# Thirty-two batches of unread one-pass products behind the first 32 rows of a modulation matrix

## The reference

```python
c_act = jax.nn.silu(c)
mod = c_act @ ada_w[l] + ada_b[l]
sh1, sc1, g1, sh2, sc2, g2 = jnp.split(mod, N_MOD, axis=-1)
h = rms_norm(x, mix_pre_g[l]) * (1.0 + sc1[:, None, :]) + sh1[:, None, :]
y = hybrid_mixer(h, w_in[l], conv_w[l], ...)
x = x + g1[:, None, :] * rms_norm(y, mix_post_g[l])
h = rms_norm(x, ffn_pre_g[l]) * (1.0 + sc2[:, None, :]) + sh2[:, None, :]
y = swiglu_ffn(h, w_gate[l], w_up[l], w_down[l])
x = x + g2[:, None, :] * rms_norm(y, ffn_post_g[l])
```

## Time and profile before

| | |
|---|---|
| median of 2 runs | 2617.11 us (2616.35 to 2617.87) |
| span of the profiled execution | 2614.0 us |
| TensorE matmul busy | 2567.3 us, 98% |
| VectorE, ScalarE, GpSimd busy | 1691.6, 1222.0, 49.9 us |
| read from HBM | 541.78 MB, mean 208 GB/s |

### The profile page before, as it was taken

One profiled execution on the slowest core, in us unless ns is written; L12 is line 12 of the kernel. 1 busy time (PEld: TensorE's weight loads), 2 busy tenths in 40 slices (PEclk: granted clock), 3 DMA queues, 4 the chain that ended last, 5 costly groups with the idle time before them and its releaser, 6 DMA issues.

```text
span 2614.0 us, 54085 instructions
## 1 busy us (share of the span) xinstructions
PE 2567.3 (98%) x21414; PEld 2438.5 (93%) x21414; DVE 1691.6 (65%) x2347; ACT 1222.0 (47%) x1667; POOL 49.9 (2%) x98
## 2 busy tenths in 40 slices
PE   5999999999999999999999999999999999999999
PEld 1488889999999999999999999999999999999999
DVE  1388867686666666557655655554766776666667
ACT  1343455554444444446545444444544444444445
POOL 0000000000000000000000000000000000000000
PEclk9899999999999999999999999999999999999999
DMA  9988868466666666554544455555455555555554
GB/s 390 383 322 306 289 210 311 168 204 226 224 226 225 226 224 209 183 192 161 170 145 139 151 176 179 188 178 187 151 187 186 188 187 185 187 186 188 186 186 138
DMA packets 136065, 545.53 MB, mean 209 GB/s; under 512 B 15121, under 2 KB 15377, under 8 KB 123537
## 3 DMA queue, kind: packets, MB, share of 16 engines
q1 hardware_dynamic: 126288, 474.08, 54.1%
q0 software_dynamic: 9216, 67.11, 7.2%
q10 hardware_dynamic: 448, 2.75, 0.3%
HBM read 541.78 MB, written 2.10 MB: 208 GB/s over the span
## 4 chain that ended last, share of the span: by engine, by line
PE 94%; DMA 2%; DVE 2%; ACT 1%; issue 0%; ACTq 0%; DVEq 0%; SPq 0%
PE bank L1797 20%; PE bank L1799 20%; PE bank L1798 20%; PE bank L1943 9%; PE bank L1945 9%; PE bank L1944 9%; PE bank L1833 2%; DMA ada_pre<-in_ada_w 2%; PE bank L1883 1%; PE bank L1854 1%; DVE w_lo L1086 1%; ACT w_hi L540 1%; DMA bf<-in_f_bias 1%; PE bank L1901 1%; PE bank L1893 0%
## 5 line engine op out<-in xcount | busy, mean ns | idle before, releaser
L1086 DVE TENSOR_TENSOR w_lo<-raw,w_hi 128x1024 fp32r<-128x1024 f32 x836 | 1014.5, 1224 | 655.3 <-ACT w_hi L540 654.3
L540 ACT ACTIVATE w_hi<-raw 128x1024 fp32r<-128x1024 f32 x836 | 875.1, 1058 | 869.8 <-PE bank L1799 502.2
L1797 PE MATMUL bank<-h_hi,w_hi 128*128 128x258 f32 (+2 forms) x2832 | 803.4, 284 | 2.4 <-DVE tg L1400 0.8
L1798 PE MATMUL bank<-h_lo,w_hi 128*128 128x258 f32 (+2 forms) x2832 | 797.7, 282 | 0.0
L1799 PE MATMUL bank<-h_hi,w_lo 128*128 128x258 f32 (+2 forms) x2832 | 797.6, 282 | 0.0
L1797 PEld LDWEIGHTS bank<-h_hi,w_hi 128*128 128x128 f32 x2832 | 533.0, 188 | 19.0 <-issue 16.5
L1798 PEld LDWEIGHTS bank<-h_lo,w_hi 128*128 128x128 f32 x2832 | 533.1, 188 | 0.8 <-issue 0.7
L1799 PEld LDWEIGHTS bank<-h_hi,w_lo 128*128 128x128 f32 x2832 | 533.0, 188 | 0.0
L1943 PE MATMUL bank<-hid_hi,w_hi 128*128 128x256 f32 x1280 | 353.9, 276 | 0.0
L1944 PE MATMUL bank<-hid_lo,w_hi 128*128 128x256 f32 x1280 | 353.6, 276 | 0.0
L1945 PE MATMUL bank<-hid_hi,w_lo 128*128 128x256 f32 x1280 | 353.6, 276 | 0.0
(11 more groups left out here) (263 smaller groups left out, 3094.8 us busy)
## 6 DMA issues: line engine op xcount, KB each, us to landing
raw<-in_w_in SPq DMA_DIRECT2D x208, 512.0 KB, 4.3
raw<-in_w_ffn_up SPq DMA_DIRECT2D x176, 512.0 KB, 4.3
ada_raw<-in_ada_w POOLq DMA_DIRECT2D x64, 1024.0 KB, 7.1
raw<-in_w_gate SPq DMA_DIRECT2D x88, 512.0 KB, 4.2
raw<-in_w_up SPq DMA_DIRECT2D x88, 512.0 KB, 3.5
raw<-in_w_down SPq DMA_DIRECT2D x88, 512.0 KB, 4.1
raw<-in_w_ffn_down SPq DMA_DIRECT2D x88, 512.0 KB, 4.4
ada_pre<-in_ada_w SPq DMA_DIRECT2D x32, 1024.0 KB, 8.5
```

What stands on the lines that cost most here:

```text
L540: act.activation(w_hi[:, slot], raw[:, slot], ACT.Copy).then_inc(hi_ready, 1)
L1086: dve.tensor_tensor(w_lo[:, slot], raw[:, slot], fp(w_hi[:, slot]), ALU.subtract).then_inc(lo_ready, 1)
L1797: pe.matmul(dst, wh, x_hi(kt), start=first and k == 0, stop=False)
L1798: pe.matmul(dst, wh, x_lo(kt), start=False, stop=False)
```

## The change

Two float32r tensors are placed, `trial` (128 x 7168, region r2 from 0) and `trial2` (128 x 1024, region r3 from 0). GpSimd fills both with 0.5 ahead of all its other memsets, and TensorE waits for both (`trial_ready`) before it begins. Behind the ada products of each of the 32 rows, and ahead of that row's channel sum or `keep_busy`, comes one entry of `TRIALS`: 12 one-pass products (8 in row 24, 380 in all) of 128 x 128 weights by 256 to 512 moving columns, written to banks 0 and 1, which nothing reads.

The entries differ in where and how the operands lie. By row: plain ones (`unread`) in 0 to 2, 15 to 20 and 31; moving operand in pieces of 2 to 64 elements with gaps as wide (`mixed`) in 3 to 7 and 30; weights spaced by 2 or 4 elements (`spaced`) in 8 to 10; moving operand backwards (`back`) in 11 to 14; weights in the other region (`remote`) in 21 to 25; other pieces (`pieces`) in 26 to 29. The moving widths are 256 in rows 0 to 8, 10, 11 and 29; 258 in rows 9, 12, 13, 15 to 20, 22, 23, 27 and 28; 260 in row 26; 320 in rows 14, 21, 25, 30 and 31; 512 in row 24.

```diff
@@ -231,6 +231,8 @@
         rel_lo = place("rel_lo", "r3", 24608 + 4 * QSUM, [HEADS, QSUM], f32r)
         ga_s = place("ga_s", "r3", 20480, [128, 2, LIVE])
         gp_s = place("gp_s", "r3", 20480 + 2064, [128, 2, LIVE])
+        trial = place("trial", "r2", 0, [128, 7168], f32r)
+        trial2 = place("trial2", "r3", 0, [128, 1024], f32r)
         pcol = sb("pcol", [128, 7, 128])
         cwt = sb("cwt", [128, AT, CONV_K])
         ident = sb("ident", [128, 128])
@@ -272,6 +274,7 @@
         c_loaded, rows_loaded = sem("c_loaded"), sem("rows_loaded")
         consts = sem("consts")
         cact_ready = sem("cact_ready")
+        trial_ready = sem("trial_ready")
         pre_loaded = [sem(f"pre_loaded{n}") for n in range(4)]
         pre_used = sem("pre_used")
         ada_loaded = [sem(f"ada_loaded{n}") for n in range(ADA_RING)]
@@ -463,6 +466,8 @@
 
         @block.gpsimd
         def _(gp):
+            gp.memset(fp(trial[:, :]), 0.5).then_inc(trial_ready, 1)
+            gp.memset(fp(trial2[:, :]), 0.5).then_inc(trial_ready, 1)
             gp.memset(ident[:, :], 0.0).then_inc(consts, 1)
             gp.memset(ones[:, :], 1.0).then_inc(consts, 1)
             gp.memset(eps[:, 0:1], 1e-6).then_inc(consts, 1)
@@ -1854,12 +1859,76 @@
                     pe.matmul(bank[:, B_V, :], ident[:, :], pcol[:, 3:7, :].rearrange("p a n -> p (a n)"),
                               start=True, stop=True)
 
+            off = (-(base + region["r2"]) % 256) // 4
+
+            def unread(width, moving=192, weights=0, to=0, step=0, count=12):
+
+                for m in range(count):
+                    w0 = off + weights // 4 + 128 * (m % 4)
+                    m0 = off + 1024 + moving // 4 + step * (m % 4)
+                    pe.matmul(bank[:, m % 2, to:to + width], trial[:, w0:w0 + 128], trial[:, m0:m0 + width],
+                              start=True, stop=True)
+
+            def mixed(width, size, weights=128, count=12):
+
+                for m in range(count):
+                    x = trial[:, off:off + 2 * width].rearrange("p (n a c) -> p n a c", a=2, c=size)[:, :, 0]
+                    w0 = off + 2048 + weights // 4 + 128 * (m % 4)
+                    pe.matmul(bank[:, m % 2, 0:width], trial[:, w0:w0 + 128], x, start=True, stop=True)
+
+            def spaced(width, moving, step, weights=128, count=12):
+
+                for m in range(count):
+                    w0 = off + 2048 + weights // 4 + 128 * (m % 4)
+                    x0 = off + moving // 4
+                    pe.matmul(bank[:, m % 2, 0:width], trial[:, w0:w0 + 128 * step:step], trial[:, x0:x0 + width],
+                              start=True, stop=True)
+
+            def back(width, moving, weights=128, count=12):
+
+                for m in range(count):
+                    w0 = off + 2048 + weights // 4 + 128 * (m % 4)
+                    x0 = off + 64 + moving // 4
+                    pe.matmul(bank[:, m % 2, 0:width], trial[:, w0:w0 + 128],
+                              trial[:, x0:x0 + width][:, ::-1], start=True, stop=True)
+
+            far = (-(base + region["r3"]) % 256) // 4
+
+            def remote(width, moving, weights, same=False, count=12):
+
+                for m in range(count):
+                    w0 = far + weights // 4 + (0 if same else 128 * (m % 4))
+                    x0 = off + moving // 4
+                    pe.matmul(bank[:, m % 2, 0:width], trial2[:, w0:w0 + 128], trial[:, x0:x0 + width],
+                              start=True, stop=True)
+
+            def pieces(n, size, step, moving, count=12):
+
+                for m in range(count):
+                    w0 = off + 4096 + 32 + 128 * (m % 4)
+                    x0 = off + moving // 4
+                    x = trial[:, x0:x0 + n * step].rearrange("p (n c) -> p n c", c=step)[:, :, 0:size]
+                    pe.matmul(bank[:, m % 2, 0:n * size], trial[:, w0:w0 + 128], x, start=True, stop=True)
+
+            TRIALS = [(unread, (256, 64, 128)), (unread, (256, 64, 128)), (unread, (256, 64, 128)),
+                      (mixed, (256, 2)), (mixed, (256, 4)), (mixed, (256, 16)), (mixed, (256, 32)),
+                      (mixed, (256, 64)), (spaced, (256, 64, 2)), (spaced, (258, 120, 2)), (spaced, (256, 64, 4)),
+                      (back, (256, 64)), (back, (258, 120)), (back, (258, 64)), (back, (320, 64)),
+                      (unread, (258, 120, 8)), (unread, (258, 120, 32)), (unread, (258, 120, 64)),
+                      (unread, (258, 120, 192)), (unread, (258, 8, 64)), (unread, (258, 120, 120)),
+                      (remote, (320, 64, 128)), (remote, (258, 120, 128)), (remote, (258, 64, 128)),
+                      (remote, (512, 64, 128, False, 8)), (remote, (320, 64, 128, True)), (pieces, (2, 130, 192, 0)),
+                      (pieces, (129, 2, 2, 120)), (pieces, (3, 86, 128, 64)), (pieces, (128, 2, 4, 0)),
+                      (mixed, (320, 64)), (unread, (320, 64, 128))]
+            pe.wait_ge(trial_ready, 2)
             pe.wait_ge(consts, 5)
             pe.wait_ge(cact_ready, 1)
             for n, b in enumerate((B_S, B_P)):
                 for kt in range(KT):
                     pe.wait_ge(pre_loaded[kt % 4], 16 * (4 * n + kt // 4 + 1))
                     ada_products(ada_pre, kt % 4, kt, b).then_inc(pre_used, 1)
+                    form, args = TRIALS[KT * n + kt]
+                    form(*args)
                     if n == 0:
                         channel_sum(kt, SEQ)
                     elif kt >= KT - 5:
```

## The result

The changed kernel takes 2642.24 us (2642.14 to 2642.35, two runs) against 2617.11: +25.1 us, ratio 1.0096 with the interval 1.0067 to 1.0125. A later series gave 2640.97 (2640.43 to 2643.12) against 2617.02 (2613.89 to 2619.37), +24.0. The forecast was 2640, and the change is under 2%, as forecast. The total came out right. Several of its terms did not: within the start stage those that were too high sum to 3.4 us and those too low to 5.4, so that part of the agreement is luck.

A forecast was written before the change was run, and what follows sets the result against it. TensorE was taken to bound the kernel behind the start stage, where the second `turn_rows` would come 23.3 us later: 2614.0 + 23.3 = 2637.3 span, plus 3.1 to the median, 2640 us. Range 2630 to 2664.

The forecast's parts named there:

- What bounds: Behind the start stage TensorE sets the time, so any delay of the first projection comes out at the end in full.
- GpSimd: Start: the new memsets take 7.1 us, hidden before TensorE's first row lands at 12.52, with 3.7 us to spare.
- Row 1: Start stage: row 0's batch fits in the wait for the square even at low clock, so row 1 starts at 18.78.
- the other case: Start stage: row 0's batch running at the full clock, which would start row 1 0.5 us earlier.
- Plain prices: Start stage: a batch of 12 one-pass products costs 1.36 us at 256 columns, 1.43 at 258, 1.70 at 320.
- (a): Per row, one more change between product kinds costs 0.17 us; at worst 0.35 (+5.6 us), at best free (-5.3).
- another way: Start stage cross-check: 46.6 us of batches plus 5.3 of changes of kind, 28.6 of these 51.9 going into slack.
- Odd kinds (b): Seventeen batches of unusual operand layout, 24.2 us together, cost nothing extra; half speed, up to 2664, had chance 0.15.
- The turn: Row 16 starts 4.08 us after row 15's channel sum at 66.2, so at 70.3, as ScalarE's work still stands between.
- The sum: Start stage: row 15's sum at 66.2, row 16 at 70.3, then 30.0 and 18.8: second `turn_rows` at 119.0, 23.3 later.
- The 3.1 us: Whole program: the median lies 3.1 us over the profiled span, which the change leaves, so 2637.3 becomes 2640.
- Rival 2: Odd batches fall to several-pass cost, almost four times: over 2% slower, above 2669, 2713 if all 17; chance 0.08.

The follow-up runs named there:

- the repeat: The changed kernel, unaltered, run again beside the kernel before in a later series: 2640.97 us, +24.0.
- the one kernel made to test it: The changed kernel with batches behind rows 0 to 7 alone and plain rows after: 2620.84 us, +4.7, ratio 1.0020 against the kernel before.

## Why the prediction was right, point by point

- **What bounds.** Right. Behind `turn_rows` nothing changed: 126.31 - 121.10 = 5.21, and 100.90 - 95.69 = 5.21. From the projection's start to the end of the span the changed kernel took 2514.3 us and before 2513.1. I had said that a longer rest would mean a missed term; the repeat has 2513.1 again, and the other kernels with batches 2512.1 to 2513.6, so the 1.2 is a difference between executions.
- **GpSimd.** Right; 6.07 + 0.95 us of memsets, and free.
- **Row 1** was put at 18.78 and came at 17.97. Judged by the durations, the clock was up by the end of row 0's batch, which I had named as the other case. -0.8. In the repeat that batch took longer (2.8 us, against 2.2 and 0.9 of waiting), and row 1 still came at 18.05.
- **Plain prices.** The batch of 12 at 256 columns added 21.01 - 17.97 - 1.63 = 1.41 us, where 1.36 + 0.17 was expected. The step that failed is (a): a third change of kind costs 0.01 to 0.05 ahead of a channel sum or `keep_busy`, not 0.17. Over rows 1 to 15 that is -1.8 and over rows 27 to 31 (3.49 a row against 3.65) -0.8. In rows 16 to 26, with two changes, 2.63 was measured and 2.64 expected. The cross-check by "another way" was none: those rows have two new changes each, so the changes added 7.3 us in the sum and not 5.3, and the 28.6 of slack was only what remained.
- **Odd kinds (b).** Taken as free; 14 of 17 were, three ran at half speed: +1.3 + 1.4 + 1.3. I named half speed as a rival for some or all of them, and cited for 16 of them the rule of the Trainium skill (Advanced Engine Details and Errata, Memory Cachelines). The trace agrees with it on the weights spaced by 4 (one hit, 2.91 us) and differs on pieces of 2 (two hits, 2.81 and 2.82 us instead of 1.52). The measurement decides: two hits to a line of moving float32r data are half speed here. Of the 24.2 us kept for the range 4.0 came due.
- **The turn.** 66.29 to 70.39 is 4.10, expected 4.08. But I carried over the full clock of before's row 16 with it. Before came out of this gap at full clock; the changed kernel fell to the 1.2 GHz level behind it, +1.4. That the low clock would not come, since TensorE waits for no row, overlooked the one wait that remains.
- **The sum.** -0.8 - 1.8 + 2.7 puts row 15 where it was forecast (66.29 against 66.2); -0.8 + 1.4 + 1.3 makes rows 16 to 31 last 50.7 instead of 48.8. The stage grew by 25.4, forecast 23.3. Errors of -0.8, -1.8 and -0.8 stand against +2.7, +1.3 and +1.4. That they met within 2 us is in part luck.
- **Around the span.** The 3.1 us were mis-sized. In each of the later kernels the profiled execution's own time is 1.7 to 1.9 over its span. If the same holds for before's, it was about 1.3 faster than the median. So the span grew by 26.6, which is 25.4 in the stage and 1.2 behind it, and the medians by 25.1.
- **What the rows should show.** The DMA share was 0.92, not under 0.9, and the granted clock from 20 to 110 us 0.98, not 1.00. Rival 2 would have shown 0.45 a product; the cap at half speed excludes it for every moving pattern tried.

## What to carry to other kernels

In this kernel, work put behind a load was free only while two things held: the row stayed under the pace of the loads, and TensorE never fell further behind them than the ring is deep; beyond that the loads stood still, and as far as the one kernel made to test it shows, the lost time did not come back. A float32r operand of TensorE was cheap as long as its runs filled whole 16 byte lines, or nearly. For other patterns of 256 columns or so, count lines, times 1.67 to 1.75 ns, for each operand by itself, and compare with columns times 0.44 ns (0.113 us at 256); for moving data stop at twice the plain price. A short wait ahead of dense work can cost about its own length again, since the low clock may follow it. And a sum that comes out right can hold errors of both signs, so check its terms against the timeline before trusting them elsewhere.

## What was not expected of the hardware

- Moving float32r data in pieces of 2 of every 4 elements: 0.224 us for 256 columns against 0.113. Pieces of 4 shifted by one element do the same. No moving pattern of 256 columns beside plain weights cost more than 0.235 (0.454 at 512 columns), every 8th element included.
- For weights one element to a line costs more than two: 128 weights on 64 lines are free beside 256 moving columns (0.115), on 96 lines a product takes 0.169 to 0.173, on 128 lines 0.223 to 0.240. Beside 512 moving columns, 0.226 by themselves, those on 128 lines are not quite hidden: 0.250.
- Reversed moving data, weights from the other region and starts of 120 bytes past a multiple of 256 cost nothing: 1.52 to 1.55 us a batch in rows 11 to 13 and 15, 1.62 to 1.64 in rows 22 and 23 against 1.63 in rows 17 and 18.
- In the kernels with batches around it, a gap of 2.4 us was followed by the 1.2 GHz level and one of 0.68 was not; the cost was 1.5 to 3.1 us.
- Rows of 1 MB land 2.49 us apart in the stream, but now and then 4.1, with the transfers at full pace (36.86 to 40.94 in the kernel without products).
